# Four edits to the linear attention and recurrent mixer of a hybrid decoder trunk: 16-channel blocks in two products, split recurrent gates, a reordered level, a split output statistic

## The reference

```python
# layer 0
q, k, v, g_out, gk_lr, lru_x, lru_gate = split(h @ w_in)      # gk_lr has 16 channels
gk = log_sigmoid(gk_lr @ gk_w2 + gk_b) / 16
o  = gla_chunked(q, k, v, gk)
o  = rms_norm(o, gla_g) * silu(g_out)                         # mean of o*o over 128 channels: the output statistic
xr = causal_dwconv(lru_x)
r  = sigmoid(xr_block @ w_a_block + b_a);  i = sigmoid(xr_block @ w_x_block + b_x)   # recurrent gates
y  = scan(a(r), i * xr) * gelu(lru_gate)
mixed = concat(o, y) @ w_out
# layer 1
qkv, z, b_logit, a_logit = split(h @ w_in)                    # the two logits have 8 channels each
```

## Time and profile before

| | |
|---|---|
| median of 3 runs | 2987.41 us (2987.4 to 2992.82) |
| profiled execution | 2987.45 us, span 2985.6 us |
| PE matmul busy | 2932.8 us, 98% |
| PE weight load busy | 2410.8 us, 81% |
| DVE busy | 2109.6 us, 71% |
| ACT busy | 1440.2 us, 48% |
| POOL busy | 838.8 us, 28% |

### The profile page before, as it was taken

The page is one execution under the profiler, slowest core; times in us unless marked ns, Lnnn a source line. Parts: engine busy times, 40 slices in busy tenths (PEclk is TensorE's granted clock), DMA queues, the critical chain, the costliest instruction groups (busy, mean ns, idle before and its releaser), DMA issues.

```text
span 2985.6 us, 44648 instructions
## 1 busy us (share of the span) xinstructions
PE 2932.8 (98%) x16876; PEld 2410.8 (81%) x16876; DVE 2109.6 (71%) x2902; ACT 1440.2 (48%) x2651; POOL 838.8 (28%) x808
## 2 busy tenths in 40 slices
PE   8999999999999999999999999999999999999999
PEld 7788888887888778887888788878888788877886
DVE  8375638547788877778978666644754778897776
ACT  4435545335777721225433566644534677762222
POOL 4629400000566633330000122200000056663333
PEclk9999999999999999999999999999999999999999
DMA  6730231002566786533344313123100356677653
GB/s 215 249 97 22 102 125 57 29 29 99 211 245 246 268 340 245 207 122 136 138 155 153 106 58 115 57 71 113 43 29 30 140 199 252 247 295 289 254 205 134
DMA packets 198561, 457.33 MB, mean 153 GB/s; under 512 B 13792, under 2 KB 71408, under 8 KB 196464
## 3 DMA queue, kind: packets, MB, share of 16 engines
q1 hardware_dynamic: 159120, 414.32, 38.7%
q10 hardware_dynamic: 39264, 40.64, 4.0%
HBM read 304.96 MB, written 149.95 MB: 152 GB/s over the span
## 4 chain that ended last, share of the span: by engine, by line
PE 84%; DVE 9%; DMA 2%; ACT 2%; issue 2%; POOL 0%; ACTq 0%; DVEq 0%; SPq 0%; POOLq 0%
PE ps L3354 21%; PE ps L3584 10%; PE ps L3585 10%; PE ps L3586 10%; PE ps L3370 7%; PE ps L3824 3%; PE ps L3826 3%; PE ps L3825 3%; PE ps L3859 2%; PE ps L3753 2%; PE ps L3426 1%; DVE work L2158 1%; DMA wraw<-wstream_dram 1%; PE ps L3990 1%; DVE hres L2189 1%
## 5 line engine op out<-in xcount | busy, mean ns | idle before, releaser
L3354 PE MATMUL ps<-act,whi 128*128 128x512 f32 x2384 | 747.5, 395 | 3.7 <-DVE act L2179 2.9
L3354 PEld LDWEIGHTS ps<-act,whi 128*128 128x128 f32 x2384 | 444.0, 188 | 109.5 <-issue 11.3
L3354 PE MATMUL ps<-act,wlo 128*128 128x512 f32 x1192 | 464.5, 390 | 0.0
L2142 DVE TENSOR_TENSOR wlo<-wraw,whi 128x1024 fp32r<-128x1024 f32 x255 | 320.9, 1260 | 197.6 <-ACT whi L1143 164.2
L1023 POOL TENSOR_TENSOR stagedf<-quads 128x1024 f32<-128x1024 f32 x28 | 73.7, 2632 | 1047.6 <-ACTq L1434 1047.6
L2607 DVE TENSOR_TENSOR work<-work,ps 128x512 f32<-128x512 f32 x360 | 239.3, 683 | 128.2 <-PE ps L3586 124.8
L1495 ACT ACTIVATE whi<-wraw 128x1024 fp32r<-128x1024 f32 x112 | 115.8, 1056 | 369.6 <-POOL wraw L1042 307.7
L3354 PEld LDWEIGHTS ps<-act,wlo 128*128 128x128 f32 x1192 | 223.8, 188 | 47.2
L3584 PE MATMUL ps<-act,whi 128*128 128x512 f32 x624 | 244.7, 392 | 1.4 <-DVE work L2607 1.0
L3586 PE MATMUL ps<-act,wlo 128*128 128x512 f32 x624 | 243.0, 389 | 0.0
L1143 ACT ACTIVATE whi<-wraw 128x1024 fp32r<-128x1024 f32 x124 | 130.4, 1056 | 154.6 <-DMA wraw<-wstream_dram 151.7
(11 more groups left out here) (449 smaller groups left out, 7166.8 us busy)
## 6 DMA issues: line engine op xcount, KB each, us to landing
wraw<-wstream_dram SPq DMA_DIRECT2D x248, 512.0 KB, 3.6
hid_store<-staged SPq DMA_DIRECT2D x168, 512.0 KB, 3.3
act<-hid_store SPq DMA_DIRECT2D x36, 1024.0 KB, 10.9
hresr<-hid_store SPq DMA_DIRECT2D x56, 512.0 KB, 10.6
qkvz<-work ACTq DMA_DIRECT2D x32, 512.0 KB, 2.7
work<-qkvz ACTq DMA_DIRECT2D x64, 256.0 KB, 3.1
act<-hid_store SPq DMA_DIRECT2D x30, 512.0 KB, 10.7
presum<-wstream_dram SPq DMA_DIRECT2D x48, 256.0 KB, 4.3
```

The lines of the kernel that those rows point to most:

```text
L2142: TT(wlo[s][:], wraw[s][:], whi[s][:].bitcast(F32), ALU.subtract).then_inc(w_split, 1)
L3354: last = mm(out_of(u)[:, 0:width], (wlo if hl else whi)[s][:, at:at + P], rhs(kt, xp, e), start=kt == hl == xp == 0, stop=kt == kts - 1 an ...
```

## The change

1. The two blocks with 16 real channels (`narrow`) hold six copies of these channels. The lo part of the weight is written over every second copy inside `whi`, so that two products (hi part and lo part of the input) give all terms: 32 matmuls in place of 48. DVE's remainder covers 3×16 of each 128 columns. In `mixer1` DVE adds the two column groups of the logits.
2. The recurrent gates become three fp32r products each. ACT makes the hi parts of `lru_w` and of the four convolved blocks (after the gelu of each), DVE the lo parts. The `gk_w2` product becomes one fp32r product over 96 rows, for which ACT and DVE split the 16 channels too; `gk_w2` is loaded six times.
3. In the GLA loop pair 3 follows pair 2 directly.
4. The output statistic of chunks 0 to 6 is two fp32r products with a rounded matrix of ones; ACT copies the hi part of the squares, and DVE subtracts the lo part (`square_low`) after `select(c, 3)`. The last chunk's is unchanged.

```diff
@@ PE
+                terms = ((0, 0), (0, 1)) if n in narrow else ((0, 0), (0, 1), (1, 0))
                 for kt in range(KT):
-                    for hl, xp in ((0, 0), (0, 1), (1, 0)):
+                    for hl, xp in terms:
...
             def output_stat(c):
-                eng.wait_ge(o_sq, c + 1)
-                mm(bank(6), ones, sq[:], start=True, stop=True).then_inc(o_stat, 1)
+                if c < NCH - 1:
+                    eng.wait_ge(o_sq, 2 * c + 2)
+                    mm(bank(6), ones_r[:], o_sqr[:, 0, :], start=True, stop=False)
+                    mm(bank(6), ones_r[:], o_sqr[:, 1, :], start=False, stop=True).then_inc(o_stat, 1)
+                else:
+                    eng.wait_ge(o_sq, 2 * c + 1)
+                    mm(bank(6), ones, sq[:], start=True, stop=True).then_inc(o_stat, 1)
...
-                eng.wait_ge(lruw_in, 32)
                 for t in range(LRU_T):
-                    eng.wait_ge(lru_conv, t + 1)
+                    eng.wait_ge(lru_ready, 2 + t + 1)
                     for k in range(2):
...
-                            last = mm(out_of(u)[:, at], w, unit(t)[:, at], start=True, stop=True)
+                        for hl, xp in ((0, 0), (0, 1), (1, 0)):
+                            for at in E:
+                                last = mm(out_of(u)[:, at], lru_weight(hl)[:, w], lru_part_of(t, xp)[:, at], start=hl == xp == 0,
+                                          stop=hl == 1)
...
                         pair(c, 2)
+                        pair(c, 3)
                         if more:
                             gate(c + 1, (0, 1, 2, 3))
                         token_major(c)
                         if c:
                             output_stat(c - 1)
-                        pair(c, 3)
@@ ACT
                     A(unit(4 + t), unit(4 + t), ACT.Gelu_apprx_tanh).then_inc(gate_ready, 1)
+                    if t == 0:
+                        eng.wait_ge(lruw_in, 16 * 7)
+                        A(lru_weight(0), unit(10), ACT.Copy).then_inc(lru_hi, 1)
+                        A(gk_w2r[0:3 * GK_ROWS], small[0:3 * GK_ROWS, 0:256], ACT.Copy).then_inc(lru_hi, 1)
+                    eng.wait_ge(lru_conv, t + 1)
+                    A(lru_part_of(t, 0), unit(t), ACT.Copy).then_inc(lru_hi, 1)
                 nc.scalar.preload_act_table_set("sigmoid_and_others")
                 splits(ua + 8)
                 eng.wait_ge(evac, ua + 9)
+                A(gk_parts[0:3 * GK_ROWS], unit(11)[0:3 * GK_ROWS], ACT.Copy).then_inc(lru_hi, 1)
...
-                    A(sq[:], bank(6), ACT.Square).then_inc(o_sq, 1)
+                    square = A(sq[:], bank(6), ACT.Square)
+                    if c < NCH - 1:
+                        link(square)
+                        square = A(o_sqr[:, 0, :], sq[:], ACT.Copy)
+                    square.then_inc(o_sq, 1)
@@ DVE
                     scaled(ua + 4 + t, unit(4 + t))
+                    if t == 0:
+                        eng.wait_ge(lru_hi, 1)
+                        TT(lru_weight(1), unit(10), lru_weight(0).bitcast(F32), ALU.subtract).then_inc(lru_ready, 1)
...
+                    eng.wait_ge(lru_hi, 2 + t + 1)
+                    TT(lru_part_of(t, 1), unit(t), lru_part_of(t, 0).bitcast(F32), ALU.subtract).then_inc(lru_ready, 1)
                 evacuate(ua + 8, unit(11))
+                eng.wait_ge(lru_hi, 2 + LRU_T + 1)
+                low = gk_parts[GK_ROWS:2 * GK_ROWS]
+                TT(low, unit(11)[GK_ROWS:2 * GK_ROWS], low.bitcast(F32), ALU.subtract).then_inc(lru_ready, 1)
...
+                def square_low(c):
+
+                    eng.wait_ge(o_sq, 2 * c + 1)
+                    TT(o_sqr[:, 1, :], sq[:], o_sqr[:, 0, :].bitcast(F32), ALU.subtract).then_inc(o_sq, 1)
...
                     select(c, 3)
+                    if c:
+                        square_low(c - 1)
                     decayed_queries(c)
...
-                V.tensor_copy(grid(0, 16), heads_of(bank(4, 2))[:, :, 0:16]).then_inc(ba_dve, 1)
+                link(V.tensor_copy(grid(0, 16), heads_of(bank(4, 2))[:, :, 16:32]))
+                TT(grid(0, 16), heads_of(bank(4, 2))[:, :, 0:16], grid(0, 16), ALU.add).then_inc(ba_dve, 1)
```

More of the change, by code:

```diff
@@ L39 @@
 GLA_GATE_NORM = 16.0
+GLA_RANK = 16
 GDN_H = 8
@@ L343, in build @@
         workr = place("workr", WORK, [P, 20, SEQ], F32R)
+        gk_w2r = place("gk_w2r", 129024, [P, 2 * P], F32R)
+        lru_whi = place("lru_whi", 7 * UNIT, [P, SEQ], F32R)
+        o_sqr = place("o_sqr", WORK + 20 * UNIT, [P, 2, HALF], F32R)
+        ones_r = place("ones_r", WORK + 21 * UNIT, [P, P], F32R)
         presum = [place(f"presum{k}", WORK + 20 * UNIT + k * UNIT, [P, 4, HALF // 2], F32) for k in range(3)]
@@ L774, in _ @@
             sp.dma_start(unit(10), lru_w).then_inc(lruw_in, 16)
-            sp.dma_start(small[0:16, 0:256], gk_w2).then_inc(lruw_in, 16)
+            for k in range(6):
+                sp.dma_start(small[GLA_RANK * k:GLA_RANK * (k + 1), 0:256], gk_w2).then_inc(lruw_in, 16)
             sp.dma_start(unit(14, 2), masks_in.rearrange("p m n -> p (m n)")).then_inc(mask_in, 16)
@@ L1737, in gate @@
                     A(bank(7), gla["sig"], ACT.Exp, scale=-1.0).then_inc(sig_ready, 1)
+                for step in (0, 2, 3):
+                    eng.wait_ge(ops_in[1][step], 16 * PRESUMS // 3)
+                A(ones_r[:], ones, ACT.Copy)
                 for c in range(2):
@@ L3682, in mixer0 @@
                     eng.wait_ge(evac, plan.need[u] + 1)
[L3683 to L3686, removed]
+                    for at in E:
+                        last = mm(out_of(u)[:, at], gk_w2r[0:3 * GK_ROWS, hp * P:(hp + 1) * P], gk_parts[0:3 * GK_ROWS, at],
+                                  start=True, stop=True)
                     last.then_inc(unit_done, 1)
@@ L3767, in mixer0 @@
                         eng.wait_ge(gsel.sem, gsel.at("L2", NCH - 1))
-                        units([(n, u), (n + 1, u + 1)], 0, ready=lambda kt: (lru_ready, kt + 1), only=(0, 1))
+                        units([(n, u), (n + 1, u + 1)], 0, ready=lambda kt: (lru_ready, LRU_OPS + kt + 1), only=(0, 1))
                     if c:
@@ L4118, in block @@
         full = np.zeros((D, P), w.dtype)
-        full[:, :w.shape[1]] = w
+        copies = 6 if w.shape[1] == GLA_RANK else 1
+        full[:, :copies * w.shape[1]] = np.tile(w, (1, copies))
         return full.reshape(KT, P, P).transpose(1, 0, 2).reshape(P, D)
```

35 lines of the change are left out of this document (27 added, 8 removed).

## The result

| | before | after |
|---|---|---|
| median (18 runs each) | 2989.33 us (2986.08 to 2994.38) | 2995.60 us (2986.78 to 3007.38) |
| ratio, 95% interval | | 1.0022 (1.0013 to 1.003) |
| profiled execution | 2987.45 us | 2986.78 us, span 2985.0 us |

The change makes the kernel 0.22% slower, by 6.3 us in the median. But its profiled execution is 0.7 us shorter than that of before, and within 0.4 us of the forecast. The spread says that these are not two views of one number: the kernel before moved by 8 us from run to run, the changed one by 21.

What follows compares the result with a forecast made beforehand. PE, 98% busy, was taken to bound the GLA chunks, but ACT to release mixer0's end and DVE to bound mixer1. Terms -0.9 - 1.9 + 0.3 + 1.5 = -1.0 on 2987.45 gave 2986.4 us, range 2978 to 2991.

Steps and rivals of the forecast that it cites:

- part 2: GLA loop: statistics -2.5, chunk 0 -0.5, last chunk +1.1, together -1.9 us; bounds -4.1 and +1.6.
- 0.7 us to spare: GLA loop: `square_low` ends at +9.5, PE reaches the statistic at +10.2 us after a chunk's first matmul.
- the rival on this side: GLA loop: `square_low` comes late in every chunk, 1.7 us later; loop +5.8, total 2994.1 us; chance 8%.
- Mixer0: Recurrent gates: PE saves 9.8 us, but ACT's evacuations release `mix0b`, which starts 0.9 us earlier; bounds -2.3 and +0.5.
- a rival: More half-clock stretches behind mixer0's wait and the last chunk's: +1.4 and +1.7, total 2989.5 us; chance 10%.
- doesn't move: Mixer0: the weight block that a DMA delivers to ACT at 111.5 keeps its time, set by SP's queue.
- The loop's gain: GLA loop: -1.9 us in all; of it pair 3 fills PE's 0.46 us wait in chunk 0.
- The split statistic: GLA loop: two fp32r products save 0.42 us per statistic, 2.5 over chunks 1 to 6.
- The last chunk's wait: End of the GLA loop: the statistic waits 2.25 us in place of 0.58; output of chunk 7 +1.1 us.
- Mixer1: First block of `mix1b`: PE's 3.6 us saving becomes a 4 us wait, DVE's queue +0.3; bounds -3.6 and +2.0.
- The +1.5: Mixer1: clock loss behind PE's 4 us wait, taken as +1.5 us from 1.7.
- The sum: Whole kernel: -0.9 - 1.9 + 0.3 + 1.5 = -1.0 us, 2986.4 us; 55% within 2983 to 2988.5.

Runs made afterwards that it cites:

- e1: The changed kernel run again with no edit: median 2995.32 us (2984.14 to 3007.04), ratio 1.0018 to the kernel before; profiled execution 3007.04 us.
- e2: Only the change's GLA loop edits, mixer0 and mixer1 as in the kernel before: median 2990.36 us, ratio 1.0003.
- e12: e7 with DVE's evacuation of the ninth block moved ahead of the low part of convolved block 3: median 2985.99 us, ratio 0.9987 to the kernel before.
- e3: Only the change's mixer0 edits, loop and mixer1 as in the kernel before: median 2987.65 us, ratio 0.9993.
- e8: The kernel before with only pair 3 placed directly behind pair 2: median 2985.05 us, ratio 0.9984.
- e4: Only the change's mixer1 edits, everything ahead as in the kernel before: median 2989.28 us, ratio 1.0003.
- e6: The kernel before plus a spare DVE subtraction with two SBUF operands in each chunk after the first, result unread: median 2999.13 us, ratio 1.0032.
- e5: The changed kernel with ACT squaring in place in PSUM and square_low subtracting from there: median 2986.38 us, ratio 0.9989 to the kernel before.
- e10: Only the GLA loop of e7, mixer0 and mixer1 as in the kernel before: median 2982.18 us, ratio 0.9976.
- e7: e5 with chunk 6's statistic left in float32, so six chunks are split: median 2983.83 us, ratio 0.9979 to the kernel before.
- e11: e7 with mixer1 as in the kernel before: median 2983.43 us, ratio 0.9971 to the kernel before.
- e9: The changed kernel with POOL's subtractions for the next-but-one chunk waiting for square_low: median 2990.19 us, ratio 1.0005 to the kernel before.

## Why the prediction was wrong

**The step that failed** is in part 2: "`square_low` about 0.69, to +9.5", with 0.7 us to spare. The length was taken from the earlier trace rows, DVE operations of 512 columns beside a busy POOL, and the rival on this side was held down by the same sentence: "DVE's 512-column operations take 0.69 with POOL busy". Those rows read `work<-ps,work`: one of their operands lies in PSUM. `square_low` has both in SBUF, as I wrote myself in the rival, and no such DVE operation stood in the loop before. Measured: 0.69 to 6.32 us. The rival had the right place (8%) and the wrong shape. It spoke of 1.7 us in every chunk, 2994.1 in all. What the profiles of long runs (e1, e2) show is a hold-up of 4.6 to 5.6 us in two chunks (e1: 20.8 us for chunk 2, 248.63 to 269.45, and 20.3 for chunk 4, where 13.30 is a chunk without a wait), and at most 1.4 in the others; that the other long runs are of this kind is inferred from their times.

**Mixer0** was right in this profile: -0.9 forecast, -1.24 measured, the wait of 2.75 for 3.0 us. The half clock behind it, which I had left for a rival, came in that profile; in e1, behind a wait of 3.02 us, it did not. That ACT behind the DMA's block sets `mix0b` held, as e12 shows; that the block's time "doesn't move" did not. Over the eight profiles with this part ACT takes it between 108.07 and 112.17, and `mix0b` starts between 124.18 and 130.05, where six profiles without it have 128.0 to 128.9. So the size of the gain was luck of one execution, and e3's -2.1 us can't be told from none.

**The loop's gain** was undersized. I gave the level order 0.46 us in chunk 0 and nothing elsewhere. In e8 chunk 0 takes 10.83 us (222.23 to 233.06) where it took 13.51 (222.58 to 236.09), with this first pair of gate matmuls for the 1.10 us of the earlier trace rows:

```profile
226.68 0.72 PE L3794 MATMUL ps<-act,whi 128*128 128x512 f32 x2
```

About 1 us of this is the order's: with the order of before, chunk 0 takes 11.7 to 11.9 us in e3, e4 and e6. The other 1.6 us are a half-clock stretch in the profile of before, which the earlier trace rows shows and I passed over. It is not ruled out by the new order: e1 and e2 have it and take 12.75 and 13.16. In each further chunk e8 shows 0.32 us. Together that is some 3 of the 4.5 us of e8's median; what the rest is stays open. Before, pair 3 stood between the statistic and the gate block, and 1.09 us passed from its start to the gate's; directly behind pair 2 both pairs together take 1.98 (278.76 to 280.74 in e8). One border fewer between products of 64 and of 128 rows is the difference that the rows show; that the border itself costs it is argued only. The split statistic gave 0.44 for 0.42 (13.74 to 13.30). The last chunk's wait was 2.39 for 2.25.

**Mixer1** was right in its main point, 3.6 us turned into 3.66 of waits and +0.33 for DVE's queue, and wrong in the details: three short waits instead of one of 4 us, and no clock lost behind them in the first profile nor in e4's. The +1.5 did not come.

**The sum** came out right for this one execution (2986.4 for 2986.78), largely by luck. From the loop's first pair to the output of chunk 7 it took 108.70 us (221.61 to 330.31) where the kernel before took 109.77 (222.58 to the earlier trace rows's 332.35): -1.1 instead of -1.9. Two larger misses partly cancel in it. Chunks 0 to 6 gained 3.8 us (94.03 against 97.87) for 3.0 forecast, 2.4 of them in chunk 0, in spite of the statistic waits of 0.63 and 1.69; and the last chunk lost 2.8 us (14.67 against 11.90) for 1.1, because the half-clock stretch that I had left to a rival came behind its wait. Mixer1's +1.8 was +0.3. The median lies 9 us above. By e5 those 9 us are the second SBUF operand: one operand moved, 2986.38.

**A rule beside the rows.** The page SBUF — State Buffer of the Trainium skill, section SBUF: two separate sides, says that a DVE operation with two SBUF inputs and a GpSimd operation that reads SBUF exclude each other for a whole instruction, whichever starts first. The trace agrees on who is concerned: 0.69 us in all seven with one operand in PSUM. It also agrees on chunk 6 of the first profile, where 2.93 us stand beside one POOL operation of 2.35. It goes beyond it on how long: a loser that waits for one of the short POOL operations would lose 0.4 to 0.7 us, and this one lost 5.6 (6.32 - 0.69), through 14 of them.

**Open.** Why DVE is let in after one POOL operation in one chunk and after 14 in another: it started 0.24 us before POOL's next operation in a short case of e6 and 0.31 before it in a long one, but there is a short one at 0.34 in e1. Open too is why the weight block of layer 0's MLP comes 2.8 us later relative to PE in e1 than in the first profile, which makes the 4.31 us wait there; no run was made for it.

## What to carry to other kernels

Before adding an operation beside a busy GpSimd, look where its operands lie, not at its size: a subtraction of two SBUF tiles cost 0.7 or 6 us here, the same subtraction with one operand in PSUM 0.69 every time. Take a duration only from a row with the same memories on both sides of its arrow. And when a change spreads the runs, profile it until a long run is caught: the first profile here showed the fault only in a mild form, a wait of 1.69 us. The version to keep is e10, the reordered level and six split statistics with the low part from PSUM, 0.24% faster than before (0.15 to 0.33%); e7 and e11, with more of the change, can't be told from it.

## What the runs showed of the hardware that was not expected

- A DVE operation with two SBUF operands was held up through as many as 14 back-to-back POOL operations (5.6 us), while POOL's kept their 0.40 us; it was let in as POOL's train ended (e9), and in e1 with no pause of POOL.
- The harm doesn't need a consumer: e6's spare operation delayed what stood behind it on DVE, and cost 9.6 us in the median.
- Putting a product of 64-row tiles directly behind another saved 0.32 us per chunk, in which nothing had waited (e8, 13.74 against 14.06).
